# A decoder block with 64 experts: shared products spread over waits, a table stored column by column, weight buffers released by halves, and one load moved ahead

## The reference

```
scores = sigmoid(x @ w_router)                    # 512 tokens x 64 experts
pick the 4 best of 8 groups, then the 8 best experts of them for each token
w = chosen scores / their sum * 2.5
for each expert e, for each token t that chose it:
    y[t] += (silu(x[t] @ w_gate[e]) * (x[t] @ w_up[e])) @ w_down[e] * w[t, e]
y += (silu(x @ ws_gate) * (x @ ws_up)) @ ws_down   # the shared expert
```

## Time and profile before

| | |
|---|---|
| median of 3 runs | 1160.64 us (1160.28 to 1162.89) |
| the profiled run's own time | 1159.71 us |
| its span | 1157.9 us |
| busy: PE, PE's weight loads, DVE, ACT, POOL | 1090.7, 632.2, 462.6, 285.4, 282.0 us |
| moved by DMA | 307.83 MB, mean 266 GB/s |
| mean granted clock of PE | 0.981 |

### The profile page before, as it was taken

How to read it: one execution, slowest core, us unless ns; L and a number is a source line. 1 busy time by engine, 2 the same in 40 slices (tenths; PEclk the granted TensorE clock), 3 DMA queues, 4 the chain that set the end, 5 groups by cost and what they waited for, 6 DMA issues and landing times.

```text
span 1157.9 us, 19667 instructions
## 1 busy us (share of the span) xinstructions
PE 1090.7 (94%) x7927; PEld 632.2 (55%) x7928; DVE 462.6 (40%) x1032; ACT 285.4 (25%) x653; POOL 282.0 (24%) x210
## 2 busy tenths in 40 slices
PE   6999999999998989899999999999899989999796
PEld 5888787767776879644333333333333333333375
DVE  5445645545536743643222342121121211111787
ACT  5023333333335510131111111111111111111623
POOL 4522624342333421010111111111111202110043
PEclk9999999999998989989999999999999989999999
DMA  9711212111112433596999999999999999998771
GB/s 370 268 37 37 73 56 74 55 56 55 56 37 78 159 120 146 217 363 265 416 426 426 426 425 423 422 420 417 408 423 418 420 396 425 419 381 317 313 318 73
DMA packets 49370, 307.83 MB, mean 266 GB/s; under 512 B 10240, under 2 KB 11136, under 8 KB 30976
## 3 DMA queue, kind: packets, MB, share of 16 engines
q1 hardware_dynamic: 37472, 273.00, 58.5%
q0 software_dynamic: 11808, 33.57, 7.3%
HBM read 290.28 MB, written 25.69 MB: 273 GB/s over the span
## 4 chain that ended last, share of the span: by engine, by line
PE 70%; DMA 19%; issue 5%; DVE 3%; POOLq 1%; POOL 1%; DVEq 0%; SPq 0%; ACT 0%
PE bank L1536 17%; PE bank L462 16%; DMA sb_gate_up<-in_w_gate_up 15%; PE bank L1560 7%; PE bank L1119 4%; PE bank L1109 4%; PE bank L471 3%; PE bank L495 3%; DMA sb_down<-in_w_down 3%; PE bank L526 3%; PE bank L508 2%; PE bank L1526 2%; PE bank L1146 2%; PE bank L1086 1%; PE bank L548 1%
## 5 line engine op out<-in xcount | busy, mean ns | idle before, releaser
L1536 PE MATMUL bank<-sb_gate_up,sb_xgT 128*32 128x512 f32 (+1 forms) x2384 | 298.1, 606 | 18.0 <-DMA sb_gate_up<-in_w_gate_up 17.9
L462 PE MATMUL bank<-sb_x_hl,sb_w_hl 128*128 128x512 f32 x768 | 191.8, 403 | 9.5 <-DVE sb_x_hl L588 9.5
L1536 PEld LDWEIGHTS bank<-sb_gate_up,sb_xgT 128*32 128x32 f32 (+1 forms) x2384 | 89.5, 115 | 195.0 <-issue 191.4
L462 PEld LDWEIGHTS bank<-sb_x_hl,sb_w_hl 128*128 128x128 f32 x768 | 142.5, 191 | 56.0 <-issue 16.1
L1560 PE MATMUL bank<-sb_down,sb_work 128*32 128x512 f32 (+1 forms) x1192 | 149.3, 595 | 4.8 <-DMA sb_down<-in_w_down 3.1
L1621 POOL DMA_INDIRECT expert_rows<-sb_rows_out,sb_work x41 | 42.6, 1038 | 453.4 <-DVE sb_rows_out L1697 453.4
L263 POOL TENSOR_TENSOR sb_w_hl<-sb_r,sb_w_hl 128x1024 fp32r<-128x1024 f32 x52 | 126.5, 2437 | 68.2 <-ACT sb_w_hl L1242 45.3
L1707 DVE TENSOR_TENSOR sb_work<-sb_work,bank 128x256 f32<-128x256 f32 x41 | 17.3, 422 | 267.3 <-ACT sb_work L1743 267.3
L1743 ACT ACTIVATE sb_work<-bank 128x256 f32<-128x256 f32 x41 | 15.8, 384 | 296.4 <-PE bank L1536 296.4
L1560 PEld LDWEIGHTS bank<-sb_down,sb_work 128*32 128x32 f32 (+1 forms) x1192 | 44.0, 112 | 81.7 <-issue 78.2
L672 DVE CUSTOM_DVE_ANT_0 sb_h<-bank,sb_bias 128x128 f32<-128x128 f32 (+3 forms) x96 | 43.4, 488 | 112.3 <-PE bank L495 111.7
(11 more groups left out here) (255 smaller groups left out, 1305.0 us busy)
## 6 DMA issues: line engine op xcount, KB each, us to landing
sb_gate_up<-in_w_gate_up SPq DMA_DIRECT2D x62, 2048.0 KB
sb_down<-in_w_down SPq DMA_DIRECT2D x64, 1024.0 KB
sb_r<-in_w_front SPq DMA_DIRECT2D x54, 512.0 KB, 3.6
sb_rows<-expert_rows SPq DMA_DIRECT2D x6, 2048.0 KB, 16.5
sb_gateT<-in_cmp_w SPq DMA_DIRECT2D x2, 2048.0 KB, 14.3
sb_gate_up<-in_w_gate_up SPq DMA_DIRECT2D x4, 1024.0 KB
sb_rows<-expert_rows SPq DMA_DIRECT2D x3, 1024.0 KB, 8.5
sb_y<-in_x_T SPq DMA_DIRECT2D x4, 512.0 KB, 6.8
```

The costliest lines, as they stand in the source:

```text
L462: last = nc.tensor.matmul(out[:, :], w6_hl[:, slot_at[n], zw, k, :], x_hl[:, zx, k, :], start=k + i == 0, stop=k == KD - 1 and i == 2)
L1536: last = nc.tensor.matmul(bank[BH][rows, :], xgT[:, k, rows], gate_up[slot_of[r]][:, :, k, :], start=k == 0, stop=k == KD - 1)
```

## The change

Five things are changed. (1) PE's 24 shared products are issued as 4, 1, 1, 4, 1 and 13, the single ones after the mask products, after the turning of the weights, and between the lists of steps 1 and 2. (2) `tokw` is laid out by column, tile and expert rather than by expert, tile and column: the writers' elements are neighbours, a list's six are not. (3) The gate/up weights lie in HBM and in their homes by chunk of the depth, gate and up side by side, so that a half of a home is four chunks of both; in the first four steps PE signals the fourth chunk (`gu_half`), and SP loads the freed homes' first halves on that signal and the second ones at the end of the products. (4) SP issues the first expert's gate/up load after `wo_done`, ahead of the wait for the last normed tile and its store. (5) In the steps the lists go to other places: 4 and 5 after step 0's gate/up products, 6 after the next rows, 7 after the shared products, 8 and 9 in step 1; the transposes of tiles 2 and 3 stand before step 0.

```diff
@@ -868,13 +868,14 @@
...
         IN_HALVES = (4, 5)
+        HALF_STEPS = 4
         slot_of, landed_at, landed_gu, before, holder = {}, {}, {}, {}, {}
...
             landed_at[r] = 16 + (landed_at[before[r]] if r in before else 0)
-            landed_gu[r] = (32 if x in IN_HALVES else 16) + (landed_gu[before[r]] if r in before else 0)
+            landed_gu[r] = (32 if x in IN_HALVES or r in before and last_step[before[r]] < HALF_STEPS else 16) + (landed_gu[before[r]] if r in before else 0)
             slot_of[r], holder[v] = BUFFER[v], r
@@ -883,7 +884,7 @@
...
         LIST = 6
-        tokw = wk(NE * NT * LIST // 2).bitcast(BF16).rearrange("p (a b c) -> p a b c", a=NE, b=NT)
+        tokw = wk(NE * NT * LIST // 2).bitcast(BF16).rearrange("p (c t e) -> p c t e", c=LIST, t=NT)
         wts = wk(NS)
@@ -926,7 +927,9 @@
...
         shared_order = [v for s in range(2 * NT) for v in shared_in[s]]
-        lists_in = {0: [4, 5, 6], 1: [7, 8, 9]}
+
+        LISTS_IN = {0: ([4], [5], [6], [7]), 1: ([8], [], [9], [])}
+        lists_in = lambda s: LISTS_IN.get(s, ([], [], [s + LEAD] if s + LEAD < NS else [], []))
         jcmp = sb("overflow_ends", place["dist"][0], [P, 16, NE])[:, :, :]
@@ -965,14 +968,14 @@
...
 
-            return tokw[:, :, :, 3 + c].rearrange("p e t -> p t e")
+            return tokw[:, 3 + c, :, :]
 
...
                 for t in range(NT):
-                    last = nc.tensor.matmul(out[rows, :], hot_of(s)[:, t, rows], tokw[:, r, t, :], start=t == 0, stop=t == NT - 1)
+                    last = nc.tensor.matmul(out[rows, :], hot_of(s)[:, t, rows], tokw[:, :, t, r], start=t == 0, stop=t == NT - 1)
             last.then_inc(E["list"], 1)
@@ -1035,10 +1038,11 @@
...
             for t in range(NT):
+                if t == NT - 1:
+                    sp.wait_ge(M["wo_done"], 4 * NT)
+                    load_gate_up(sp, 0, 0)
                 sp.wait_ge(M["xn"], t + 1)
                 sp.dma_start(xn2_d[t * P:(t + 1) * P, :], y[:, t, :]).then_inc(M["stored"], 16)
-            sp.wait_ge(M["wo_done"], 4 * NT)
-            load_gate_up(sp, 0, 0)
             load_down(sp, 0, 0)
@@ -1178,9 +1182,14 @@
...
 
-            others = [(t, k) for k in range(4) for t in range(1, NT)]
-            for t, k in others[:3]:
-                shared_up(t, (k,))
+            others = [(t, k) for k in range(4) for t in range(1, NT)] + [(t, k) for t in range(1, NT) for k in range(4, KD)]
+
+            def more_of_shared(n):
+                for t, k in others[:n]:
+                    shared_up(t, (k,))
+                del others[:n]
+
+            more_of_shared(4)
 
@@ -1191,10 +1200,12 @@
...
             last.then_inc(M["listing_pe"], 1)
+            more_of_shared(1)
             pe.wait_ge(*LISTING["wn"])
...
             last.then_inc(M["listing_pe"], 1)
+            more_of_shared(1)
             pe.wait_ge(*LISTING["perm"])
@@ -1216,20 +1227,19 @@
...
             last.then_inc(M["listing_pe"], 1)
-            for t, k in others[3:8]:
-                shared_up(t, (k,))
+            more_of_shared(4)
 
...
             pe.wait_ge(*LISTING["part2"])
-            for s in range(4):
+            for s in range(2):
                 list_rows(s)
-            for t, k in others[8:]:
-                shared_up(t, (k,))
-            for t in range(1, NT):
-                shared_up(t, range(4, KD))
+            more_of_shared(1)
+            for s in range(2, 4):
+                list_rows(s)
+            more_of_shared(len(others))
             for t in range(2):
@@ -1313,8 +1323,8 @@
...
                 nc.vector.tensor_copy(v16, v)
-            nc.vector.tensor_copy(tokw[:, :, :, 0], C["tok_a"].unsqueeze(1).to_broadcast([P, NE, NT]))
-            nc.vector.tensor_copy(tokw[:, :, :, 1], C["tok_b"].unsqueeze(1).to_broadcast([P, NE, NT]))
+            nc.vector.tensor_copy(tokw[:, 0], C["tok_a"].unsqueeze(2).to_broadcast([P, NT, NE]))
+            nc.vector.tensor_copy(tokw[:, 1], C["tok_b"].unsqueeze(2).to_broadcast([P, NT, NE]))
             for t in range(NT):
@@ -1414,7 +1424,7 @@
...
             dve.wait_ge(*LISTING["before_pe"])
-            nc.vector.tensor_scalar(tokw[:, :, :, 2].rearrange("p e t -> p t e"), psv(7, NT, NE), 1.0, None, ALU.subtract)
+            nc.vector.tensor_scalar(tokw[:, 2], psv(7, NT, NE), 1.0, None, ALU.subtract)
             dve.drain()
@@ -1526,14 +1536,16 @@
...
 
-        gate_up = [v.rearrange("p i (k n) -> p i k n", k=KD) for v in raw]
+        gate_up = [v.rearrange("p a (k i n) -> p (a k) i n", i=2, n=EH) for v in raw]
 
...
                     rows = slice(row, row + n)
-                    last = nc.tensor.matmul(bank[BH][rows, :], xgT[:, k, rows], gate_up[slot_of[r]][:, :, k, :], start=k == 0, stop=k == KD - 1)
+                    last = nc.tensor.matmul(bank[BH][rows, :], xgT[:, k, rows], gate_up[slot_of[r]][:, k, :, :], start=k == 0, stop=k == KD - 1)
+                if k == KD // 2 - 1 and s < HALF_STEPS:
+                    last.then_inc(M["gu_half"], 1)
             last.then_inc(E["gu"], 1)
@@ -1591,7 +1603,24 @@
...
                 half_of_gate_up(x, 1)
-            for _, _, x, what in loads:
+            for s in range(HALF_STEPS):
+                freed = [x for p, phase, x, what in loads if p == s and what == "gate_up"]
+                for x in freed:
+                    number(x)
+                for i in range(2):
+                    if i == 0:
+                        sp.wait_ge(M["gu_half"], s + 2)
+                    else:
+                        sp.wait_ge(E["gu"], s + 1)
+                    for x in freed:
+                        half_of_gate_up(x, i)
+                for p, phase, x, what in loads:
+                    if p == s and what == "down":
+                        sp.wait_ge(E["dn"], p)
+                        load_down(sp, expert[x], load_order[x])
+            for p, _, x, what in loads:
+                if p < HALF_STEPS:
+                    continue
                 r = load_order[x]
@@ -1651,28 +1680,26 @@
...
             move_rows(0)
-            pe.wait_ge(M["hid"], NT)
+            for t in range(2, NT):
+                shared_transposes(pe, t)
             pe.wait_ge(M["hT"], 2)
...
                         pe.wait_ge(s_raw[slot_of[r]], landed_gu[r])
-                now = lists_in.get(s, [s + LEAD] if s + LEAD < NS else [])
-                for n in now[:-2]:
-                    list_rows(n)
+                behind_first, behind_turned, behind_rows, behind_shared = lists_in(s)
                 gate_up_products(s)
-                if s == 0:
-                    for t in range(2, NT):
-                        shared_transposes(pe, t)
-                for n in now[-2:-1]:
+                for n in behind_first + behind_turned:
                     list_rows(n)
...
                     move_rows(s + 1)
-                for n in now[-1:]:
+                for n in behind_rows:
                     list_rows(n)
...
                     shared_down(pe, *v)
+                for n in behind_shared:
+                    list_rows(n)
                 if s == NS - 1:
@@ -1698,10 +1725,10 @@
...
             for s in range(NS):
-                for n in lists_in.get(s, [s + LEAD] if s + LEAD < NS else []):
+                if s == 1:
+                    take_lists(dve, 1, bank[BL][:, 4 * LIST:8 * LIST])
+                for n in [n for part in lists_in(s) for n in part]:
                     one_hot(dve, n)
-                    if s < 2 and n == GROUPS[n // 4][-1]:
-                        take_lists(dve, n // 4, bank[BL][:, 4 * LIST * (n // 4 % 2):4 * LIST * (n // 4 % 2) + 4 * LIST])
                 n = s + LEAD
@@ -1738,12 +1765,11 @@
...
             rows_in(0)
+            for t in range(2, NT):
+                shared_turned(act, t)
             for s in range(NS):
...
                 nc.scalar.activation(sg, bank[BH][:, 0:EH], ACT.Silu).then_inc(E["silu"], 1)
-                if s == 0:
-                    for t in range(2, NT):
-                        shared_turned(act, t)
                 if s + 1 < NS:
@@ -2153,7 +2179,7 @@
...
     arrays["in_ws_gate_up"] = np.stack([np.asarray(inputs[n])[0].reshape(KD, P, EH).transpose(1, 0, 2) for n in ("ws_gate", "ws_up")], axis=2).reshape(P, -1)
-    arrays["in_w_gate_up"] = np.concatenate([np.asarray(inputs[n]).reshape(NE, P, KD * EH) for n in ("w_gate", "w_up")], axis=2)
+    arrays["in_w_gate_up"] = np.stack([np.asarray(inputs[n]).reshape(NE, P, KD, EH) for n in ("w_gate", "w_up")], axis=3).reshape(NE, P, -1)
     a = {n[3:]: nc.dram_tensor(n, v.shape, mybir.dt.from_np(v.dtype), kind="ExternalInput").ap() for n, v in arrays.items()}
```

More of the change, by code:

```diff
@@ L1773, in build @@
         listed1, place1 = listed[:, 0, :], place4[:, 0:2]
-        wgu = raw[last6[4]].rearrange("p i (k n) -> p i k n", k=KD)
+        wgu = gate_up[last6[4]]
         def overflow_sync(sp):
@@ L1818, in overflow_tensor @@
                     for t in range(NT):
```

(4 more changed lines are left out.)

## The result

The changed kernel takes 1153.54 us (median of 6 runs, 1151.74 to 1155.85), the kernel before 1160.85 beside it. The ratio is 0.9927, with its interval [0.9911, 0.9944]: 8.5 us less, between 6.5 and 10.3. Forecast were 1150.8 us and 9.8 us less.

The account below looks back on a forecast made before the run. Weights' traffic was taken to bound the steps of experts. Idle removed 11.3, less 0.3 for the late order and 1.2 for the gap left, gave 9.8 us: 1160.6 to 1150.8 us, range 1147.5 to 1156.8.

Parts of the forecast that it names:

- The bound: The 41 steps of experts: bound by weights' traffic, 419 GB/s from 542 to 1020 us, PE waiting 21.0 us for weights.
- The idle time: DMA engines in the 42 us before 542 us: 11.3 us idle, the most to be had unless the stream starts sooner.
- traffic never out: Sign at step 1: first halves issued near 529.3 us, reaching the DMA engines just in time, before the stream runs dry.
- PE's earlier steps: Lists, shared products and step 0 come sooner, so step 1 starts at 525.7, 8.2 us sooner; the sum's rest beyond halves' 3.5.
- B: Rival: PE's start brought forward less, by slow clock, slow table writes or late first rows; gain about 7, 1153.7 us; 21%.
- D: Rival: slower, first gathers starved by SP's never empty queue; at 26 us landing 4 us slower, 1164.6 us; 4%.
- The first expert: Its load issued some 4.9 us sooner; the time returns as a gap before 493 us; gain 0, bounds 0 to 1.
- The halves: Homes given back by halves in steps 0 to 3, 3.5 us before a step's end: 3.5 us of the 9.8 gain.
- The gap left: Behind step 1's loads, before step 2's halves at 544.5 us: 1.2 us idle remains, then no more gaps.
- Rival E: Halves cost the stream 0.5 us each for seven loads, 3.4 in all: gain 6.4, 1154.2 us; 6%.
- rival C: Lead isn't kept: homes, not traffic, limit; only PE's lead counts, 8.2 at best; 1152.4 to 1154.6 us; 7%.
- A: The forecast itself: 1150.8 us, own range 1148 to 1154; 59%.

Follow-up runs that it names:

- after: The changed kernel with all five changes, against the kernel before: 1153.54 us, ratio 0.9927; run again in a later comparison, 1153.75 us, ratio 0.9929.
- whole homes: The changed kernel without release by halves: the first four steps free whole homes, as before the change; 1153.16 us, ratio 0.9929 to the kernel before.
- two with all loads split: Changed kernel, homes loaded in two transfers in all 41 steps: released by halves, ratio 0.9989; both issued once the whole home is free, 1.0002.
- shorter step 0 with halves: Changed kernel, step 0 with one list and no shared part, halves in steps 1 and 2 only: 1150.50 us, ratio 0.9905 to the kernel before.
- halves alone: The kernel before with halves of homes in the first four steps and nothing else changed: 1161.63 us, ratio 0.9999.
- products together: The changed kernel with shared products in blocks of 3, 5 and 16, as before the change: 1159.04 us, ratio 0.9980 to the kernel before.
- table by expert: The changed kernel with the token table laid out by expert, tile and column again: 1158.27 us, ratio 0.9969 to the kernel before.

## Why the prediction was right, and which step was not

**The bound.** That the steps of experts are bound by weights' traffic, and that the end moves with the stream's restart, held: PE's waits stayed (23.3 us after, 20.7 with whole homes, 21.1 when run again; 19.4 forecast), the long stretch moved as much per us as before (418 GB/s), and the gain followed PE's lead within 1.6 us over eleven runs. The two with all loads split are the exception: their long stretch moved 414 and 415 GB/s, and their tail's loads went late.

**The idle time.** The prediction counted 11.3 us of it before 542 us, from the shares, as the most to be had. Counted in bytes it is more: in the 42 us before, 12.0 MB were moved, which take 28.6 us at 419 GB/s, so 13.4 us were to be had. The shorter step 0 with halves, whose stream leads by 12 us, agrees. And the sign "traffic never out" failed, which fits: the queue ran out near 530, or 527.6 with the 2.36 off, where the prediction had 531.0, and from 530 to 534 the engines were mostly idle (0.34). The share from 500 to 535 us was to be over 0.97; it was 1.01, 0.96 and then 0.54.

**PE's earlier steps.** Each term came out: the writes (1.34 to 0.38 and 0.40 on ACT, 1.33 to 0.42 on DVE; forecast 0.37), full clock from 492 to 498.7, the lists, the end of the shared products, step 0 (landing of the first rows no problem), step 1. Two things beside it: POOL's subtraction fell from 0.98 and 1.09 to 0.64 us, where I held that its 2.3 for two stay, and the order was not 0.3 late (495.39 - 2.36 = 493.03, before 492.99). Rivals B and D fell with it.

**The first expert.** Nothing, as forecast, and by the mechanism given: between 494.0 and 496.5 the share is 0.32, a gap ahead of the order's load.

**The halves: the step that failed.** The prediction ended its sum with "9.8, of which the halves alone give 3.5 and PE's earlier steps the rest". Measured, the halves give 0.1 us alone (-1.0 to 1.2) and nothing beside PE's earlier steps, which give all of it, 8.2 us. The times of issue were right, and the traffic came out of the hole within 1 us of where I said. Three sizes were wrong:
- The gap left was put at 1.2 us, after which the stream would be continuous. The lead falls from 11.0 to 9.0 us between 70 and 80 MB, by 2.0. About 1.2 of it is the thin stretch from 544 on: what was issued early has been moved, the next half is issued at 546.36, as late as PE reaches it, and in between one down load and some rows are all there is, in packets that take longer. What a half brings forward is in part given back at the next wait.
- A load in two transfers was put at 0 of 0 to 3.4 us for seven. It is 0.10 each, 0.7 in all. I had read "share 1.00 with 1 MB loads between 2 MB ones" as no cost. The share can't show this cost: it is time in which the engines are busy at a lower rate. Rival E had the mechanism, with a size five times too large.
- PE's part alone was taken as 6.3 (9.8 - 3.5). It is 8.2, its whole lead at step 1, since with whole homes the end of step 1's products is what restarts the stream.

That is the arithmetic of rival C, "only PE's lead counts, 8.2 at best", 1152.4, to which I gave 7%, and 1153.5 lies in its range. Its reason, that from step 4 on homes come free by whole steps again, is not what was seen: most of the halves' lead is gone by 80 MB, before that could tell. The forecast of 9.8 lies within the interval of the gain (6.5 to 10.3), and so does B's 7, so by the total alone A, B and C are not told apart. That the total came near is in part luck: 3.5 too much for the halves against 1.9 too little for PE's steps. The parts are told apart: 3.5 for the halves lies outside the interval of the halves alone, and whole homes differ from after by 0.0002 of the ratio, 0.2 us, with intervals of 1.5 and 1.9 us to each side.

**What stays open.** Whether halves are worth a microsecond where later waits come sooner too is not shown: in the second profile of the change the stream's lead stays near 9.3 us to the end, whole homes have 7.9, and the times don't differ. Why 8 KB packets take longer when few transfers are in flight was not looked into. And 1.2 us of thin stretch and 0.7 of splits overlap by an unknown amount, since loads in two parts also ran at lower rates within that stretch.

## What to carry to other kernels

Where a stream of loads is held by buffers, the gain is how much sooner the consumer frees the buffer that restarts it: work on the path to that one moment (here step 1's gate/up products), and count what the idle time before it could have moved, in bytes and not by the share, only as the upper limit. Giving back a buffer in parts moves a wait rather than removing it, unless all later ones come sooner too, and each part costs a little in a full queue. A share of 1.00 doesn't say that the stream is as fast as it can be: read the GB/s beside it. And where an experiment widens a loop of waits, look at what stands behind the loop: here the tail's loads went 33 us later, and the 5.4 to 6.0 us that this cost look like a price of the halves unless the last step is timed by itself.

## What was not expected of the hardware

- Two 1 MB transfers in place of one of 2 MB cost 0.10 us in a full queue (4.4 us over 44 loads), with the share at 1.00 to 1.01 and the rate down from 419 to 414 and 415 GB/s. A packet of 8 KB took 316 ns, one of 16 KB 618.
- The same 8 KB packets took 420 ns on the mean in five us in which few transfers were in flight: share 0.97, 291 GB/s.
- An operation of POOL gets faster by the layout of its input: the subtraction of 128x256 took 0.98 and 1.09 us with bf16 elements 48 bytes apart as one input, 0.64 with dense ones.
- PE reads six bf16 elements 512 bytes apart as fast as six neighbours (0.31 and 0.30 us for the same group of list products).
- PE's clock fell to half after a thin stretch of the middle in three versions: for 6.8 us before (491.9 to 498.7), twice for 3.4 us with the products together, and once for 3.4 us with the table by expert. One product of no use in each wait kept it at 1.00.
